# A mixer's attention heads in step, products grouped by kind, and four conditioning slabs on TensorE

## The reference

```
z = q @ k^T / 8                                     # per head, 512 queries x 640 padded keys
log_keep = where(valid, -softplus(z), 0)            # valid: key < query, key is not padding
log_rest = sum of log_keep over the later keys      # reverse cumsum, exclusive
attn = where(valid, exp(log_sigmoid(z) + log_rest), 0);  out = attn @ v

S = S * w + (S @ -kk) (kk*a)^T + v k^T;  y_t = S @ r_t   # recurrence, token by token
y = group_norm(y) * lnx_w + lnx_b + (sum r*k*r_k) * v    # the last term is the "bonus"
```

## Time and profile before

| | us |
|---|---|
| median of 3 runs | 2142.86 (2141.77 to 2146.6) |
| the profiled execution | 2141.41 |
| its span | 2140.2 |
| PE busy | 1985.7 (93%), 13960 matmuls |
| DVE, ACT, POOL busy | 780.6, 702.8, 763.3 |

### The profile page before, as it was taken

One profiled execution on the slowest core, in us unless ns is written; L12 is line 12 of the kernel. 1 busy time (PEld: TensorE's weight loads), 2 busy tenths in 40 slices (PEclk: granted clock), 3 DMA queues, 4 the chain that ended last, 5 costly groups with the idle time before them and its releaser, 6 DMA issues. The chain is left out here.

```text
span 2140.2 us, 32154 instructions
## 1 busy us (share of the span) xinstructions
PE 1985.7 (93%) x13960; PEld 1672.0 (78%) x13960; DVE 780.6 (36%) x1061; ACT 702.8 (33%) x1056; POOL 763.3 (36%) x444
## 2 busy tenths in 40 slices
PE   3878989999999999999999899988999699999997
PEld 2656767778888889999999898866767478888885
DVE  6664362232211012444310166643444423444201
ACT  2553221342222233222222334354544333222222
POOL 2222121334444555444445433211110154444453
PEclk9999998999999999999999999998988999999998
DMA  7233121324323332223222422000000322332231
GB/s 275 99 118 119 60 99 31 99 69 148 126 90 94 92 100 90 90 89 99 86 87 88 130 89 74 31 6 2 2 2 2 129 74 94 99 90 97 91 97 58
DMA packets 55724, 182.76 MB, mean 85 GB/s; under 512 B 7553, under 2 KB 7809, under 8 KB 55457
## 3 DMA queue, kind: packets, MB, share of 16 engines
q1 hardware_dynamic: 55584, 180.72, 25.7%
HBM read 175.45 MB, written 5.24 MB: 84 GB/s over the span
## 5 line engine op out<-in xcount | busy, mean ns | idle before, releaser
L2093 POOL TENSOR_TENSOR WL<-RAWS,WH 128x1024 fp32r<-128x1024 f32 (+2 forms) x275 | 650.2, 2367 | 960.5 <-ACT WH L1622 960.5
L489 PE MATMUL PS<-HH,WH 128*128 128x264 f32 (+2 forms) x2184 | 669.3, 348 | 48.8 <-issue 11.5
L489 PE MATMUL PS<-HL,WH 128*128 128x264 f32 (+2 forms) x2184 | 655.3, 342 | 0.0
L489 PE MATMUL PS<-HH,WL 128*128 128x264 f32 (+2 forms) x2184 | 653.9, 341 | 0.0
L489 PEld LDWEIGHTS PS<-HH,WH 128*128 128x128 f32 (+1 forms) x2184 | 378.2, 190 | 114.5 <-issue 33.5
L1622 ACT ACTIVATE WH<-RAWS 128x1024 fp32r<-128x1024 f32 (+2 forms) x275 | 283.8, 1033 | 452.1 <-PE PS L489 396.5
L489 PEld LDWEIGHTS PS<-HL,WH 128*128 128x128 f32 (+1 forms) x2184 | 379.3, 190 | 47.8 <-issue 1.9
L489 PEld LDWEIGHTS PS<-HH,WL 128*128 128x128 f32 (+1 forms) x2184 | 378.3, 190 | 48.7 <-issue 0.6
L489 PE MATMUL PS<-IHf,WH 128*128 128x512 f32 (+1 forms) x704 | 209.4, 338 | 0.0
L489 PE MATMUL PS<-IHf,WL 128*128 128x512 f32 (+1 forms) x704 | 209.2, 338 | 0.0
L489 PE MATMUL PS<-ILf,WH 128*128 128x512 f32 (+1 forms) x704 | 209.2, 338 | 0.0
(11 more groups left out here) (491 smaller groups left out, 1900.4 us busy)
## 6 DMA issues: line engine op xcount, KB each, us to landing
RAWS<-w_w_in SPq DMA_DIRECT2D x52, 512.0 KB, 4.2
RAWS<-w_ada SPq DMA_DIRECT2D x32, 512.0 KB, 3.6
RAWS<-w_f0g SPq DMA_DIRECT2D x22, 512.0 KB, 3.6
RAWS<-w_f0u SPq DMA_DIRECT2D x22, 512.0 KB, 3.7
RAWS<-w_f1g SPq DMA_DIRECT2D x22, 512.0 KB, 3.6
RAWS<-w_f1u SPq DMA_DIRECT2D x22, 512.0 KB, 3.5
RAWS<-w_f2g SPq DMA_DIRECT2D x22, 512.0 KB, 3.5
RAWS<-w_f2u SPq DMA_DIRECT2D x22, 512.0 KB, 3.5
```

Of the source, the lines that this page charges most:

```text
L489: ins = te.matmul(ps[0:m, q, o:o + b - a] if len(halves) > 1 else ps[0:m, o:o + b - a], w[:, k * m:k * m + m], v[:, k0 + k, a:b], start=fi ...
L2093: ge.tensor_tensor(WL[s % NS][:, 0:n], RAW[i % NR][:, 0:n], WH[s % NS][:, 0:n].bitcast(f32), ALU.subtract).then_inc(*w_lo.up(s))
```

## The change

- **Conditioning.** Slabs 0 and 1 of each of the first two vectors are no longer weighted on DVE. PE multiplies them by their two columns of `silu(c)` (`ada_direct`, 64 instructions), ahead of the sums of squares, and `ada_column` adds to the same PSUM columns. DVE weighs 12 slabs in place of 16, and the pair that holds slabs 2 and 3 is loaded first. The constants come after two pairs, the meta tokens are left out here (they are loaded again later anyway), and POOL's first memsets and SP's next loads wait for the second column in place of the last accumulation.
- **Heads.** `heads()` does both heads of a pair in every step, b = 0 then b = 1. In the output products the two alternate block by block.
- **Kept sums.** Only the current block's parts and one running sum are kept. POOL adds the block before to this block's tile (`ht`), ACT and DVE make its high and low part (`upper_sum`, `lower_sum`) at columns 512 on, a round later; PE then does four sum products a round at most.
- **Order.** The merge becomes five ticks of the recurrence for every four of the heads; a round of the two heads together has ten ticks. Before, a turn had two ticks of the recurrence and one of each head stream, and a round had five.
- **Products by kind.** In `r` of a scan the eight state products come first, then the eight others, which read 64 rows of `SV` in place of 128 rows of `V0`. `V0`, its memset and its copies go. In the output part the four 128*128 products come first, then the eight 128*64.
- Group norm's two semaphores by tile become two counters. The words "late bonus" of the change's name have no lines in the diff: before already issues the bonus' product one slab late.

```diff
-ATT_TICKS = 107
+ATT_TICKS = 50
...
+    DIRECT = (0, 1)
+    WEIGHED = [j for j in range(48) if j >= 16 or j % 8 not in DIRECT]
+    ADA_PAIRS = (1, 0, 2, 3, 4, 5, 6, 7)
...
+    KAT = (512, 0, 0, 0, 0)
...
+        def ada_direct(v, b):
+            for k in DIRECT:
+                j = 8 * v + k
+                te.wait_ge(s_ad[j // 2], 16)
+                for m in range(8):
+                    te.matmul(b[:, m:m + 1], ADA[:, j, 128 * m:128 * m + 128], CA[:, k:k + 1],
+                              start=k == DIRECT[0] and m == 0, stop=False, skip_group_check=True)
...
-        te.wait_ge(s_in, 48)
-        te.wait_ge(*c_act.at("ones"))
+        te.wait_ge(*c_act.at("silu"))
+        for v in range(2):
+            ada_direct(v, bank(v))
+        te.wait_ge(s_k0, 16)
         sum_squares(0)
         ada_column(0, bank(0))
         ada_column(1, bank(1))
...
             for i in range(4):
                 for par, q in enumerate(HALF):
-                    te.matmul(PS[q, 6, 64 * i:64 * i + 64], AR[:, i, n, 0, :], SB[:, i, par, :], start=True, stop=False)
-                    ins = te.matmul(PS[q, 6, 64 * i:64 * i + 64], MM[e][:, 2 * i + par, 0:64], V0[:, 2 * i + par, :],
-                                    start=False, stop=True)
+                    te.matmul(PS[q, 6, 64 * i:64 * i + 64], AR[:, i, n, 0, :], SB[:, i, par, :], start=i == 0, stop=False,
+                              skip_group_check=True)
+            for i in range(4):
+                for par, q in enumerate(HALF):
+                    ins = te.matmul(PS[q, 6, 64 * i:64 * i + 64], MM[e][64:128, 2 * i + par, 0:64],
+                                    SV[e][64:128, 2 * i + par, :], start=False, stop=True, skip_group_check=True)
...
+                    for b, q in enumerate(HALF):
+                        te.matmul(PS[:, b, 0:n], KA[q, i, 128 * j:128 * j + 128], QA[q, i, 512 - n:512], start=True,
+                                  stop=True).then_inc(*hp[b].up("z", r))
+                    for _ in range(7):
+                        yield
+                    for b in range(2):
+                        te.wait_ge(*hd[b].at("lo", r))
                         for part in (KHI[b], KLO[b]):
+                            ins = te.matmul(PS[:, b, 0:n], TRIR[:, :], part[:, KAT[x]:KAT[x] + n], start=False, stop=True,
+                                            skip_group_check=True)
+                        if x:
+                            if x > 1:
+                                te.wait_ge(*hl.at(6 * i + 2 * x - 4 + b))
+                            m = LEN[j + 1]
+                            for part in (KHI[b], KLO[b]):
+                                ins = te.matmul(PS[:, b, n - m:n], ONER[:, :], part[:, 512:512 + m], start=False,
+                                                stop=True, skip_group_check=True)
+                        ins.then_inc(*hp[b].up("c", r))
...
                 for j in range(5):
+                    for b, q in enumerate(HALF):
+                        h = 2 * i + b
+                        ins = te.matmul(PS[q, b, 512 - LEN[j]:512], VT[:, j, 64 * h:64 * h + 64],
+                                        ATT[b][:, OFF[j]:OFF[j] + LEN[j]], start=(j == 0), stop=(j == 4))
...
-        alternate(rk, heads(0), rk, later_by(2, heads(1)))
+        rk, both = pipeline(NCH, rw_prepare, rw_scan), heads()
+        alternate(rk, both, rk, both, rk, both, rk, both, rk)
...
-        for j in range(16):
+        for j in WEIGHED[:16 - 2 * len(DIRECT)]:
...
+        def lower_sum(i, x, b):
+            n = LEN[BLOCKS[x]]
+            ve.wait_ge(*hh.at(6 * i + 2 * x - 2 + b))
+            ve.scalar_tensor_tensor(KLO[b][:, 512:512 + n], TT[b][(5 * i + x) % 2][:, 0:n], -1.0,
+                                    KHI[b][:, 512:512 + n].bitcast(f32), ALU.mult,
+                                    ALU.subtract).then_inc(*hl.up(6 * i + 2 * x - 2 + b))
...
+        def upper_sum(i, x):
+            r, n = 5 * i + x, LEN[BLOCKS[x]]
+            for b in range(2):
+                ae.wait_ge(*ht.at(6 * i + 2 * x - 2 + b))
+                ae.activation(KHI[b][:, 512:512 + n], TT[b][r % 2][:, 0:n], ACT.Copy,
+                              scale=-1.0).then_inc(*hh.up(6 * i + 2 * x - 2 + b))
...
-            ge.tensor_copy(V0[64:128, :, :], SV[e][64:128]).then_inc(*rv0.up(n))
...
+                    if x in (1, 2, 3):
+                        for b in range(2):
+                            t = TT[b][r % 2][:, 128:n]
+                            ge.wait_ge(*hd[b].at("lo", r))
+                            if x > 1:
+                                ge.wait_ge(*ht.at(6 * i + 2 * x - 4 + b))
+                            ge.tensor_tensor(t, t, TT[b][(r - 1) % 2][:, 0:n - 128],
+                                             ALU.add).then_inc(*ht.up(6 * i + 2 * x - 2 + b))
...
         se.dma_start(CV[:, :], cols).then_inc(s_in, 16)
-        se.dma_start(KC[0][:, :], consts[:, 0:NCON[0]]).then_inc(s_in, 16)
-        se.dma_start(X[:, :, 0:NM], mv).then_inc(s_in, 16)
         se.dma_start(X[:, :, NM:T2], xv).then_inc(s_x, 16)
-        for i in range(8):
+        for n, i in enumerate(ADA_PAIRS):
+            if n == 2:
+                se.dma_start(KC[0][:, :], consts[:, 0:NCON[0]]).then_inc(s_k0, 16)
             se.dma_start(ADA[:, 2 * i:2 * i + 2, :],
                          slabs["ada"][2 * i:2 * i + 2].rearrange("j p t -> p j t")).then_inc(s_ad[i], 16)
...
-        se.wait_ge(*ada_acc.at(15))
+        se.wait_ge(*ada_col.at(1))
```

More of the change, by code:

```diff
@@ L370, in program @@
     at_tr = count("at_tr")
-    rz = steps("rz", "v0", "sb")
+    rz = count("rz")
     rp = [steps(f"rp{i}", "bk", "u", "tr", *INV_PE) for i in range(2)]
@@ L393, in program @@
     gn_a = [steps(f"gn_a{i}", "sq", "ln", "exp") for i in range(4)]
-    gn_g = [count(f"gn_g{i}") for i in range(4)]
-    gn_hi = [count(f"gn_hi{i}") for i in range(4)]
+    gn_g = count("gn_g")
+    gn_hi = count("gn_hi")
     wo2_x = count("wo2_x")
@@ L925, in rw_scan, with heads @@
+                for h in range(8):
+                    i, par = divmod(h, 2)
+                    ins = te.matmul(PS[64 * par:64 * par + 64, 6, 64 * i:64 * i + 64], SV[e][:, h, :],
+                                    MM[e][:, h, 64:128], start=False, stop=True, skip_group_check=True)
                 ins.then_inc(*qy.up(n - 1))
             yield
-        def heads(b):
-            pb = 64 * b
+        def heads():
             for i in range(4):
-                h = 2 * i + b
                 for x, j in enumerate(BLOCKS):
@@ L2010, in heads @@
-                    ae.activation(t, t, ACT.Ln, bias=1.0).then_inc(*a.up("ln", r))
+                    t = [TT[b][r % 2][:, 0:n] for b in range(2)]
+                    for b in range(2):
+                        ae.wait_ge(*hp[b].at("z", r))
+                        if x >= 2:
+                            ae.wait_ge(*ht.at(6 * i + 2 * x - 4 + b))
+                        ae.activation(t[b], PS[:, b, 0:n], ACT.Abs).then_inc(*ha[b].up("abs", r))
+                    yield
+                    for b in range(2):
+                        ae.wait_ge(*ha[b].at("abs", r))
+                        ae.activation(t[b], t[b], ACT.Exp, scale=-1.0).then_inc(*ha[b].up("exp", r))
```

208 lines of the change are left out of this document (97 added, 111 removed).

## The result

The changed kernel takes 2114.66 us, median of four runs from 2114.2 to 2123.29, where the kernel before takes 2142.32 on the same chip (2135.4 to 2146.6). The ratio is 0.9887, with a 95% interval of 0.9861 to 0.9913. So 27.7 us are gone by the medians; the forecast had 30.5. The profiled execution took 2114.2 us, its span 2113.0.

The account below looks back on a forecast made before the run. The prediction took PE, busy 93% of 2140.2 us, to be the bound. Gains of 30 us in the merge and 0.5 at the start gave 2110.9 for the profiled execution, 2112.4 for the median; range 2086 to 2140.

Parts of the forecast that it names:

- PE work that goes: Merge: fewer sum products, overlapping outputs and scores, and scan products by kind take 42 us off PE.
- rival (c): Merge: long streams of two heads don't overlap, or clock low for 40% of the stage; 2132 us, chance 0.20.
- PE is no longer the bound: Merge: one chain of 20 rounds, 246 us, rivals PE work; PE idles 40 to 60 us, waiting on the low-part step.
- (d): Merge: queues couple the chains, up to 16 us a round, PE waiting before recurrence steps for DVE; 2167 us, chance 0.12.
- The clock: Merge: PE's pauses put a quarter of the stage at 1.2 GHz in place of a fifth, making 246 us 269.
- The chain: Merge: steps of a lock-step round add up to 13.6 us for 512 columns; 61.6 us by 4 is 246 us.
- some 0.6 of the recurrence's ACT work between: Merge round's chain: recurrence work on ACT between the heads' abs, exp and ln steps, 0.6 us.
- 0.8 of recurrence work on DVE in front of the low parts: Merge round's chain: recurrence steps queued on DVE ahead of the heads' low parts, 0.8 us.
- The start: First 48 us: PE's direct products of four slabs take DVE's place; gain 0.5 us, bounds -0.5 and 7.
- Behind the merge: After the merge: nothing in the diff moves, so everything shifts with the merge's end.
- (b): Merge and start: overlap works and the clock stays up, stage 250, start gains 5; 2092 us, chance 0.15.
- (e): Whole kernel: time within 0.2% of before, chance 0.03.

Follow-up runs that it names:

- full_sums: Changed kernel without the kept running sums, so a head has 2, 4, 6, 8, 10 sum products a round: 2125.68 us.
- sum_early: Changed kernel with the running sum's two parts made at the end of a round, behind the attention exponential: 2111.82 us.
- ratio_only: Kernel before with only the tick ratio changed, five of the recurrence to four of the heads: 2130.81 us.
- The early runs: Changed kernel with high and low part issued earlier, with the running sum made at round end, and with both: 2115.95, 2111.82 and 2106.54 us.
- lo_early: Changed kernel with ACT's high part one tick earlier and DVE's low part in the tick of the running sum's: 2115.95 us.
- kinds: Changed kernel with the scan's output part mixed as before instead of kind by kind: 2131.65 us.
- order_only: Kernel before with only the new order of the start's transfers, all sixteen slabs on DVE: 2137.3 us.
- outputs_apart: Changed kernel with the two heads' output products one head after the other instead of alternating: 2129.28 us.
- start_only: Kernel before with all of the change's conditioning part and nothing of the merge: 2142.4 us.
- the merge alone: Changed kernel with the conditioning of before: 2120.02 us.

## Why the prediction was right, and where it was not

**The total** of 2112.4 was 2.3 us off, by two errors that cancel: the merge gained 16.4 us for 30, the time ahead of it 10.6 for 0.5. That the total came so close is luck, and the more so as most of the 10.6 stayed away in eight kernels with the same code.

**PE work that goes: right, and a little low.** 42 us forecast, 49 less busy time measured, the clock's part in it. The two scores of a round overlap fully (1.06 us to the next start, I had taken 1.4 to 1.5 for the order of two and two); outputs 3.23 for 3.5; scan part 1.65 for 1.7. The overlap of long streams, half of rival (c), holds.

**PE is no longer the bound: right in the main.** Idle 62 us against "40 to 60", and its largest single wait is on the low part, as said: 19.0 us. But its waits for DVE ahead of recurrence steps, the sign named for (d), come to 19.2 us together. Added PE work cost 3.7 us for 10 where it stood beside the chain's waits (full_sums) and its full price in two other places.

**The clock: right in share, 24% for "a quarter".** Among kernels in lock-step it is lower where PE is idle for longer (0.90 with 52 us idle, 0.85 with 64), but sum_early (0.92 with 57) and the kernel before (0.90 with 29, where ratio_only has 0.95 with 32) show that it is no function of the idle time.

**The chain: the term that was mis-sized.** The forecast gave a group of rounds 61.6 us at full clock, 66.5 with the clock's share; it took 69.9. (The terms listed for a round of 512 columns add up to 13.4 and not 13.6, which changes this little.) By round, forecast (times 266/246) and measured mean: 8.6 and 9.7, 10.3 and 9.8, 12.1 and 13.8, 14.7 and 13.0, 15.6 and **19.0**, outputs 5.3 and 4.6. The last round's 3.4 us are as much as the whole difference; the others are off by up to 1.7 and cancel. The step that failed is "some 0.6 of the recurrence's ACT work between" and "0.8 of recurrence work on DVE in front of the low parts": it priced those instructions by their duration, when what they cost is also their wait. By the table of last rounds the max step starts 6.5 us after the score on average, where its terms up to there add up to 4.8, and from the first high part to the first low part it is 3.6 us, where the sum has 1.9 (1.1 and 0.8). At its worst, once, a state update tied to PE's scan held a finished low part up for 4.8 us, some of it by the low clock.

The early runs bear this out in part. Moving steps in DVE's and ACT's queues shortens PE's idle time by 4.8, 5.4 and 10.5 us with no work changed. They don't show that this one state update is the cause: lo_early moved the low part ahead of it and last rounds got no shorter on average, and sum_early left it there and gained 13.6 us, more than half of it in PE's busy time, which fits the clock. The Trainium skill (TensorE: Matmul & The Clock Gate, Architectural detail) has VectorE and ScalarE as strict first in, first out; the order of the rows agrees, DVE was idle in front of ready work. This is the mechanism of rival (d), at about a quarter of its strength: with its share of the outputs a round takes 14.0 us, where the forecast's 266 us make 13.3 and (d) had 16.

**The terms don't add.** Undoing single edits costs 3.7 (sums), 8.8 (outputs) and 11.2 us (kinds); the tick ratio alone gains 8.2. That is 31.9 us, and the change gives 16.4. So what is left of the change, the lock-step with its one chain, would cost about 15 us by this sum. But each of those numbers has the clock in it. At half a us for each us at 1.2 GHz the four become 9, 8, 7 and a loss of 7, together 17, and the change gives 20. By that estimate the lock-step costs nothing. No run has lock-step without the rest, so its price is open between these.

**The start: mis-sized, 0.5 forecast for 5 to 6.** Three parts. The order of the transfers was left out of the sum, though its rows were there, and is worth 3.7 us (order_only). The column sums run at 2.4 GHz in this trace, which the forecast named as the case worth 5 to 7 us. And of the 7.5 us that the columns end earlier, DVE's slower work beside POOL takes 2.3 back by its rows, which the sum did not have. The clock is no sure gain: of ten profiled kernels with the new conditioning, five have the burst of 32 in 3.7 to 4.0 us, five in 6.8, the low level, with the same code, as this row of outputs_apart:

```profile
34.39 6.83 PE L533 MATMUL PS<-KC,ACC 128*128 128x1 f32 x32
```

The first main product then stands at 42.9 to 43.4 us in the first five and at 46.1 to 47.0 in the others, where order_only, with all slabs on DVE, has 44.66. So four slabs on PE, on top of the new order, gave 1.2 to 1.8 us in half of the builds and cost 1.5 to 2.3 in the other half.

The total doesn't confirm the start: start_only is at 1.0004, order_only, a part of it, at 0.9977, and the merge alone has all but 5 us of the gain. It is worth between 0 and 5 us, and which stays open.

**Behind the merge: nothing, as said.** The late part is as long in both kernels, within 0.3 us.

**Rivals.** (b) needed a clock that stays up; it fell. (c) is out by outputs_apart. (d) was right in part on the mechanism and wrong on the size. (e) is out.

## What to carry to other kernels

When work leaves a bounding engine, list what stands in each queue ahead of every step of the new chain, and price the step by when its own producer will be done, not by how long it takes: a 0.4 us instruction that waits 3 us in front of ready work can cost up to 3 us, and how much comes back depends on what is late next (moving the low part up 4.9 us made its round 2.7 shorter). Here PE was idle for 29 to 32 us with two chains out of step and for 52 to 66 in lock-step; joining chains to save matrix work can put their waits in line, so look at once for steps that can be issued a tick earlier or made at the end of a round. Keep subtractions of two SBUF tensors on DVE away from the moment at which POOL starts an addition. And before prices of single edits are added up, look at the clock of each trace: here it changes a sum of 32 us to 17.

## What was not expected of the hardware

- Four 512-column instructions in the order head 0, head 0, head 1, head 1, on different row halves, take the time of two: 1.13 us. Overlap needed no alternation there; the outputs, on different halves of the output partitions, were tried in both orders and needed it (3.23 against 5.64).
- A DVE subtraction of 128x384 took 1.35 us beside a POOL addition and 0.56 without. In the changed kernel the two low parts of 512 columns at 1510.21 and 1511.35 took 1.22 and 1.21 us beside two POOL products, for 0.69 elsewhere. At the start one of L1075 took 2.83 us beside POOL's two, for 0.75 before.
- The same start code gave the 32 one-column sums 3.72 us in some builds and 6.83 in others, after the same 64 one-column products at 0.22 us each.
